# One latent weave re-filled, its layer norms cut into pieces, and the logits' wait on the copies narrowed, in a two-block transformer kernel on one core

## The reference

```python
def mixer_layer(x, cx, c, c_ctx, w_in, w_out, w_ada, b_ada, ln_g, ln_b, ...):
    shift, scale, gate = split(silu(c) @ w_ada + b_ada, 3)          # and the same for c_ctx
    h  = x * (1 + scale) + shift                                    # modulation, hc likewise
    (a_q, a_i, a_ff, a_fb, b_q, b_k, b_v, c_q, c_k, c_v, d_q, d_k, d_v, g_lat) = split(h @ w_in)
    y_a = hgrn2_mixer(...)       # gated linear recurrence, both directions
    y_b = global attention, normed and rotated q, k   (keys of latents and context)
    y_c = differential attention                       (the same)
    y_d = windowed attention with a sink               (the same)
    y = concat(y_a, y_b, y_c, y_d) * silu(g_lat)
    x_new = layer_norm(alpha * x + gate * (y @ w_out), ln_g, ln_b)
    # the context gets the same in the first layer only

def layer_norm(x, g, b):
    mu = mean(x); var = mean(square(x - mu))
    return (x - mu) * rsqrt(var + 1e-5) * g + b
```

## Time and profile before

| | |
|---|---|
| time, median of 3 runs | 1595.27 us (1594.75 to 1596.22) |
| the profiled execution | 1594.29 us, of which its span 1592.3 us |
| PE busy | 1465.8 us (92%), 8186 instructions |
| DVE busy | 544.5 us (34%) |
| ACT busy | 399.2 us (25%) |
| POOL busy | 145.9 us (9%) |
| mean granted TensorE clock | 0.958 of full speed |
| `two0`, first logits to last mix | 987.0 to 1231.0 us |
| end of `two0` to first projection of `two1` | 1231.0 to 1300.7 us |
| `two1` | 1300.7 us to the end of the span |

### The profile page before, as it was taken

How to read it: one execution, slowest core, us unless ns; L and a number is a source line. 1 busy time by engine, 2 the same in 40 slices (tenths; PEclk the granted TensorE clock), 3 DMA queues, 4 the chain that set the end, 5 groups by cost and what they waited for, 6 DMA issues and landing times. The chain is left out here.

```text
span 1592.3 us, 20238 instructions
## 1 busy us (share of the span) xinstructions
PE 1465.8 (92%) x8186; PEld 1186.5 (75%) x8186; DVE 544.5 (34%) x1273; ACT 399.2 (25%) x730; POOL 145.9 (9%) x191
## 2 busy tenths in 40 slices
PE   5999999999999999999999999998998969779875
PEld 2887887888878788888888887776776847556664
DVE  1352122102153233141454223355444121465331
ACT  2122122310212223333133222223333012232221
POOL 0111100000020210000110001213000001231000
PEclk9999999999999999999999999999997979889977
DMA  9544344454355444433332343542422314111100
GB/s 369 217 168 168 146 159 185 168 203 185 132 190 208 159 168 159 165 133 136 129 132 106 110 142 119 212 185 76 161 94 82 133 41 144 54 53 41 67 0 27
DMA packets 30764, 219.86 MB, mean 138 GB/s; under 512 B 3792, under 2 KB 3920, under 8 KB 4304
## 3 DMA queue, kind: packets, MB, share of 16 engines
q1 hardware_dynamic: 30672, 218.57, 37.1%
HBM read 217.51 MB, written 1.05 MB: 137 GB/s over the span
## 5 line engine op out<-in xcount | busy, mean ns | idle before, releaser
L812 PE MATMUL event<-u,ring 128*128 128x256 f32 x3200 | 722.0, 385 | 17.5 <-DVE u L1621 10.6
L812 PEld LDWEIGHTS event<-u,ring 128*128 128x128 f32 x3200 | 610.3, 193 | 121.1 <-issue 30.8
L805 PE MATMUL event<-ring,u 128*128 128x256 f32 (+1 forms) x704 | 150.6, 372 | 0.0
L805 PEld LDWEIGHTS event<-ring,u 128*128 128x128 f32 x704 | 128.6, 191 | 20.7 <-issue 4.6
L1159 ACT ACTIVATE region<-event 128x512 f32<-128x512 f32 x72 | 43.0, 597 | 317.9 <-PE event L812 317.7
L986 PE MATMUL event<-region,ring 128*128 128x256 f32 x544 | 119.1, 379 | 2.9 <-DVE region L1641 2.9
L986 PEld LDWEIGHTS event<-region,ring 128*128 128x128 f32 x544 | 102.8, 190 | 17.9 <-issue 4.2
L1195 ACT ACTIVATE S<-logits,stat 128x512 f32<-128x512 f32 (+2 forms) x160 | 83.8, 535 | 111.3 <-DVE stat L1520 92.0
L1827 POOL TENSOR_TENSOR raw<-raw,tables 128x512 f32<-128x512 f32 (+1 forms) x28 | 34.1, 1219 | 843.8 <-DVE turned L1485 530.7
L897 PE MATMUL logits<-region 64*128 64x256 f32 (+4 forms) x320 | 66.1, 515 | 36.5 <-ACT PT L1211 22.0
L961 PE MATMUL event<-region,ring 128*128 128x256 f32 x384 | 84.4, 380 | 0.0
(11 more groups left out here) (191 smaller groups left out, 1232.3 us busy)
## 6 DMA issues: line engine op xcount, KB each, us to landing
ring<-in_w SPq DMA_DIRECT2D x202, 1024.0 KB, 4.8
tables<-in_two SPq DMA_DIRECT2D x1, 1600.0 KB, 9.4
x<-in_x SPq DMA_DIRECT2D x1, 1024.0 KB, 17.6
x<-in_ctx SPq DMA_DIRECT2D x1, 1024.0 KB, 6.5
out<-x SPq DMA_DIRECT2D x1, 1024.0 KB, 3.9
tables<-in_one SPq DMA_DIRECT2D x1, 832.0 KB, 9.0
tables<-in_late SPq DMA_DIRECT2D x1, 512.0 KB, 5.7
consts<-in_common SPq DMA_DIRECT2D x1, 320.0 KB, 3.3
```

The source lines that it names most:

```text
L805: ins = mm(bank[:, t * 256:t * 256 + width], mem.u[:, q, k, t * P:(t + 1) * P], wt[:, k * 256:k * 256 + width], start=k == 0, stop=k == KB ...
L812: ins = mm(bank[:, j * 256:(j + 1) * 256], wt[:, k * 256 + j * P:k * 256 + j * P + P], mem.u[:, q, k, :], start=k == 0, stop=k == KB - 1)
```

## The change

Three parts.

**Scripts.** The fill of `two0` is laid out anew. `kk` and `vv` of the context leave the weave; `vv` now stands between `mean(0)` and `var(0)`, and `fv` and `kk` between `var(0)` and `feed(0)`, after the weave. The other projections are spread so that in the second half of the weave there is one after each logits or each turn up to logits(14). The context's layer norm and feed move from slots 7 to 11 to slots 11 to 14. The head norm of the context's keys (`sq`, `norm` of gk1) moves from slots 18 and 19 of `two0` into the start of `two1`, where the first logits now wait for it. The load of the `late` table follows `proj vv` of the context as before, and so moves with it.

**Layer norms in pieces.** The mean's matmuls wait for the four `out` drains one by one; centring and squares are four instructions of 128x512 instead of one of 128x2048, each signalled; the variance's matmuls take the squares pair by pair; the eight multiplications, the eight additions and the eight of `feed` each signal the next engine singly, and the first projection after a `feed` waits block by block. The final store is four DMAs of 256 KB, each after its two blocks.

**Logits.** `logits(n)` waits for `turns_copied` only where one of the jobs n-2 to n is of kind C (these exist in block one only).

```diff
     fill = [[] for _ in range(2 * len(jobs))]
-    for h, items in ((0, [proj("hq")]), (1, [proj("hi")]), (2, [proj("nq")]), (3, [("rot", "nq", 0)]), (4, [out(1)]), (5, [out(2)]),
-                     (6, [out(3)]), (7, [("mean", 1)]), (8, [proj("fk"), ("var", 1)]), (9, [proj("fq"), ("rot", "fk", 0)]),
-                     (10, [proj("fv"), ("rot", "fq", 0)]), (11, [("mod", "v1"), ("feed", 1, "v1")]),
-                     (12, [proj("g", 0, 0)]), (14, [proj("ff", 1)]), (15, [proj("fb", 1)]), (17, [proj("kk", 1)]),
-                     (18, [proj("hi", 1), ("sq", "gk1")]), (19, [("norm", "gk1")]), (20, [proj("g", 0, 1)]), (22, [proj("g", 0, 2)]), (24, [proj("g", 0, 3)]),
-                     (26, [proj("vv", 1)]), (28, [("silu", 0)]), (29, [("gate", 0, 0)])):
+    for h, items in ((0, [proj("hq")]), (2, [proj("nq")]), (3, [("rot", "nq", 0)]), (4, [out(1)]), (6, [proj("hi")]), (7, [out(2)]),
+                     (9, [proj("fk")]), (10, [out(3)]), (11, [("mean", 1), ("rot", "fk", 0)]), (12, [proj("fq"), ("var", 1)]),
+                     (13, [("rot", "fq", 0)]), (14, [proj("fv"), ("mod", "v1"), ("feed", 1, "v1")]), (15, [proj("ff", 1)]),
+                     (17, [proj("fb", 1)]), (19, [proj("g", 0, 0)]), (21, [proj("hi", 1)]), (23, [proj("g", 0, 1)]),
+                     (25, [proj("g", 0, 2)]), (27, [proj("g", 0, 3)]), (28, [("silu", 0)]), (29, [("gate", 0, 0)])):
         fill[h] += items
     for h, items in enumerate(latent_scan()):
         fill[3 + h] += items
-    for h, items in ((18, [("decay", 1)]), (19, [("prep", 1, "khat")]), (21, [("khatT", 1)]), (23, [("state", 1)])):
+    for h, items in ((20, [("decay", 1)]), (22, [("prep", 1, "khat")]), (24, [("khatT", 1)]), (26, [("state", 1)])):
         fill[h] += items
-    for g, h in enumerate((1, 3, 5, 7, 13, 16)):
+    for g, h in enumerate((1, 5, 8, 11, 16, 20)):
         fill[h] += group("v1", g)
         fill[h + 1].append(("ada", g, "v1"))
     s += weave(len(jobs), fill)
     s += [("sq", "f0"), proj("fk", 1), ("norm", "f0"), ("gate", 0, 1)] + [("out", i, (0,)) for i in range(4)]
-    return s + [proj("fv", 1), ("mean", 0), ("var", 0), ("feed", 0, "v1")]
+    return s + [("mean", 0), proj("vv", 1), ("var", 0), proj("fv", 1), proj("kk", 1), ("feed", 0, "v1")]
 
 
 def script_two1():
...
     s = [proj("kk"), proj("vv"), ("rot", "nk", 0), ("sq", "gk0"), proj("gq"), ("norm", "gk0"), ("sq", "gq0"), proj("ff"), proj("fb"),
-         ("rot", "gk", 0), ("norm", "gq0"), proj("hq"), ("rot", "gq", 0), ("decay", 0)]
+         ("rot", "gk", 0), ("norm", "gq0"), ("sq", "gk1"), proj("hq"), ("rot", "gq", 0), ("norm", "gk1"), ("decay", 0)]
...
 
-    eng.wait_ge(sems["x_normed"], w.at("x_normed", 0))
-    eng.dma_start(dram["out"], mem.x[:, 0, :, :]).then_inc(sems["stored"], 16)
-    eng.wait_ge(sems["stored"], 16)
+    for i in range(4):
+        eng.wait_ge(sems["x_normed"], w.at("x_normed", 2 * i + 2 - KB))
+        eng.dma_start(dram["out"][:, 2 * i:2 * i + 2, :], mem.x[:, 0, 2 * i:2 * i + 2, :]).then_inc(sems["stored"], 16)
+    eng.wait_ge(sems["stored"], 64)
...
                                 eng.wait_ge(sems["u_ready"], w.at("u_ready", k + 1))
+                            elif after is not None and j == 0:
+                                eng.wait_ge(sems["fed"], after + k + 1)
                             ins = mm(bank[:, j * 256:(j + 1) * 256], wt[:, k * 256 + j * P:k * 256 + j * P + P],
                                      mem.u[:, q, k, :], start=k == 0, stop=k == KB - 1)
...
-                fed[item[1]] = w.at("fed", sec.index(item) + 1)
+                fed[item[1]] = w.at("fed", KB * sec.index(item) + 1) - 1
...
-                eng.wait_ge(sems["turns_copied"], w.at("turns_copied", n - 1))
+                if "C" in [j.kind for j in sec.jobs[max(n - 2, 0):n + 1]]:
+                    eng.wait_ge(sems["turns_copied"], w.at("turns_copied", n - 1))
...
+                        if n == 0 and sec.name == "two1":
+                            eng.wait_ge(sems["normed"], w.at("normed", sec.index(("sq", "gk1")) + 1))
...
                 q = item[1]
-                if kind == "mean":
-                    ev = w.first[("out", 3, (q,))]
-                    eng.wait_ge(drained[ev % BANKS], w.fills(ev))
-                else:
-                    eng.wait_ge(sems["vsquares"], w.at("vsquares", sec.index(("mean", q)) + 1))
                 src = mem.x if kind == "mean" else mem.u
                 eng.wait_ge(drained[e % BANKS], w.fills(e - BANKS))
                 bank = mem.bank[e % BANKS]
                 for k in range(KB):
+                    if k % 2 == 0 and kind == "mean":
+
+                        ev = w.first[("out", k // 2, (q,))]
+                        eng.wait_ge(drained[ev % BANKS], w.fills(ev))
+                    elif k % 2 == 0:
+                        eng.wait_ge(sems["vsquares"], w.at("vsquares", 4 * sec.index(("mean", q)) + k // 2 + 1))
                     ins = mm(bank[:, 0:T], c["ones"], src[:, q, k, :], start=k == 0, stop=k == KB - 1)
                 ins.then_inc(full[e % BANKS], 1)
...
             elif kind == "mean":
-                n = sec.index(item) + 1
-                eng.wait_ge(sems["centred"], w.at("centred", n))
-                act(mem.u[:, item[1]], mem.x[:, item[1]], ACT.Square).then_inc(sems["vsquares"], 1)
+                q = item[1]
+                for i in range(4):
+                    n = 4 * sec.index(item) + i + 1
+                    two = slice(2 * i, 2 * i + 2)
+                    eng.wait_ge(sems["centred"], w.at("centred", n))
+                    act(mem.u[:, q, two, :], mem.x[:, q, two, :], ACT.Square).then_inc(sems["vsquares"], 1)
                 eng.wait_ge(sems["vsquares"], w.at("vsquares", n))
...
-                eng.wait_ge(sems["x_scaled"], w.at("x_scaled", n))
                 for k in range(KB):
                     beta = mem.par2[:, 0 if q else sec.layer, TWO_BETA + k:TWO_BETA + k + 1]
-                    ins = act(mem.x[:, q, k, :], mem.x[:, q, k, :], ACT.Identity, bias=beta)
-                ins.then_inc(sems["x_normed"], 1)
-                eng.wait_ge(sems["x_normed"], w.at("x_normed", n))
+                    eng.wait_ge(sems["x_scaled"], w.at("x_scaled", KB * (n - 1) + k + 1))
+                    act(mem.x[:, q, k, :], mem.x[:, q, k, :], ACT.Identity, bias=beta).then_inc(sems["x_normed"], 1)
+                eng.wait_ge(sems["x_normed"], w.at("x_normed", KB * n))
...
-                if tag == "v1":
-                    eng.wait_ge(sems["x_normed"], w.at("x_normed", sec.index(("var", q)) + 1))
+                n = KB * sec.index(item)
                 for k in range(KB):
-                    ins = ts(mem.u[:, q, k, :], mem.x[:, q, k, :], mod[:, KB + k, q:q + 1],
-                             mod[:, k, q:q + 1], ALU.mult, ALU.add)
-                ins.then_inc(sems["fed"], 1)
-                eng.wait_ge(sems["fed"], w.at("fed", sec.index(item) + 1))
+                    if tag == "v1":
+                        eng.wait_ge(sems["x_normed"], w.at("x_normed", KB * sec.index(("var", q)) + k + 1))
+                    ts(mem.u[:, q, k, :], mem.x[:, q, k, :], mod[:, KB + k, q:q + 1],
+                             mod[:, k, q:q + 1], ALU.mult, ALU.add).then_inc(sems["fed"], 1)
+                eng.wait_ge(sems["fed"], w.at("fed", n + KB))
...
                 eng.wait_ge(full[e % BANKS], w.fills(e))
                 ts(mem.mean[:, :], bank[:, 0:T], 1.0 / D, None, ALU.mult).then_inc(drained[e % BANKS], 1)
                 eng.wait_ge(drained[e % BANKS], w.fills(e))
-                tt(mem.x[:, q], mem.x[:, q], wide(mem.mean[:, :], KB), ALU.subtract).then_inc(sems["centred"], 1)
-                eng.wait_ge(sems["centred"], w.at("centred", n))
+                for i in range(4):
+                    two = mem.x[:, q, 2 * i:2 * i + 2, :]
+                    tt(two, two, wide(mem.mean[:, :], 2), ALU.subtract).then_inc(sems["centred"], 1)
+                eng.wait_ge(sems["centred"], w.at("centred", 4 * n))
             elif kind == "var":
                 q, n = item[1], sec.index(item) + 1
                 l = 0 if q else sec.layer
                 eng.wait_ge(sems["vrs_ready"], w.at("vrs_ready", n))
                 for k in range(KB):
-                    ins = stt(out=mem.x[:, q, k, :], in0=mem.x[:, q, k, :],
-                              scalar=mem.par2[:, l, TWO_G + k:TWO_G + k + 1], in1=mem.rs_x[:, :],
-                              op0=ALU.mult, op1=ALU.mult)
-                ins.then_inc(sems["x_scaled"], 1)
-                eng.wait_ge(sems["x_scaled"], w.at("x_scaled", n))
+                    stt(out=mem.x[:, q, k, :], in0=mem.x[:, q, k, :],
+                        scalar=mem.par2[:, l, TWO_G + k:TWO_G + k + 1], in1=mem.rs_x[:, :],
+                        op0=ALU.mult, op1=ALU.mult).then_inc(sems["x_scaled"], 1)
+                eng.wait_ge(sems["x_scaled"], w.at("x_scaled", KB * n))
 
     def pick_keys(w, qt):
 

```

10 lines of the change are left out of this document (5 added, 5 removed).

## The result

The changed kernel takes 1544.95 us (median of 4 runs, 1543.4 to 1546.11), the kernel before on the same chip 1595.01; the ratio is 0.9686, 95% interval 0.9669 to 0.9702. The profiled execution took 1544.14 us with a span of 1542.3. Of the 50.0 us that the span lost, 34.0 are idle time of PE (126.5 before, 1542.3 - 1449.8 = 92.5 now) and 16.0 are matmuls that run faster (1465.8 to 1449.8 us for the same 8186). Of the 34.0, 1.9 are scatter: PE's first matmul starts at 9.81 us before and at 7.94 now, and anywhere from 7.3 to 9.9 us in the fourteen traces.

What follows compares the result with a forecast made beforehand. TensorE, busy 92% of the span, was taken as the bound, with 126.5 us idle plus slow-clock matmuls to win. Terms 21.5 + 8 + 4 + 10.1 = 43.6 us less gave 1550.7 profiled, forecast 1551.5 us, range 1541 to 1565.

Steps and rivals of the forecast that it cites:

- A, the seam: Between `two0` and `two1`: projections placed around the layer norm's steps cover PE's stops, 21.5 us less, bounds 18.5 to 22.
- B, the weave of `two0`: New order of the fill removes stops at logits(11) and logits(15) and shortens middle ones: 8 us less, bounds -3 to 16.
- fits behind 6.9 us: In the weave of `two0`, a job's chain of maximum, exponentials and copy, about 5 us, is covered by one projection.
- The idle time that I named as a sign, near 12 us: PE's idle time expected in the weave of `two0`, with the longest stop ahead of mix(14), near 7 us.
- C, `two1`: Loosened copies' wait, less the loss from the head norm ahead of the decay: 4 us less, bounds 0 to 8.
- The loss at the start: Start of `two1`: head norm delays the decay 2.9 us, its scalings then run 1.7 us faster; net +1.2 on logits(1).
- The term that was mis-sized: In `two1`, the loosened wait gives back the copy's part of stops from logits(7) to logits(14): 4.3 us.
- D, the last layer norm: Kernel end: mean, centring, squares, additions and store in pieces overlap: 10.1 us less, bounds 7 to 12.
- the 5.7 that I took: Last layer norm, centring to variance: 5.7 of 10.7 us left, between 4.85 at 2.4 GHz and 7.75 at 1.2 GHz.
- rival 3: More clock comes back than counted, slow stretches in both weaves go too: another 5 to 8 us, 1545 us; 10%.
- Rival 2: The copies' wait only changes its name, mix or norm wait instead: 1558 us; 13%.
- Rivals 1, 4 and 5: Middle of `two0` collides, 1560 to 1566, 17%; recurrence loses step in `two0`, 1602, 1%; seam not covered, 1562, 3%.

Runs made afterwards that it cites:

- e3: The changed kernel with layer norms, feed and final store whole as before, keeping the new scripts and loosened wait: 1568.09 us.
- e1: The changed kernel with the old wait for the copies put back in front of every logits: 1563.1 us.
- e2: The kernel before with only the loosened wait of logits for the copies: 1585.29 us.
- e4: The kernel before with layer norms, feed and store in pieces, old scripts and old wait: 1573.91 us.
- e5: The changed kernel with the square and norm of gk1 right behind kk and vv in `two1`, ahead of the decay's wait: 1542.52 us.
- e8: The changed kernel with two items of slot 11 of `two0` swapped, the rotary of fk ahead of mean(1): 1546.29 us.

## Why the prediction was right, and where it was not

**A, the seam: right in size and mechanism** (21.4 for 21.5). No stop, clock 1.00, and e3 shows that the order does it without the pieces.

**B, the weave of `two0`: right sum, wrong account.** The stops in the middle came to 0.40, 2.10, 2.54, 1.47 and 0.55 us, 7.1 in all, where 7.3 were forecast, behind mean(1), variance(1) and the feed; the one at mix(14) is 6.69 where near 7 were. The step that failed is that the new order alone gives the 8, because a job's chain "fits behind 6.9 us". With the old wait, 3.7 of the 8.6 are gone (e1), with stops of 2.41 and twice 0.77 us for the copies in the new order. Without the pieces, to which the forecast gave no gain here, 5.4 are gone (e3), at the stops behind the context's layer norm. The order itself is worth 3.0 us beside the loosened wait (219.3 to 216.3, e2 to e3) and 6.4 beside the pieces (221.0 to 214.6, e4 to e1, all less vv and kk where they are in the stretch); it takes all three for the 8.6. That the sum came out is luck. The idle time that I named as a sign, near 12 us, was added up wrongly; my own 7.3 and near 7 make 14, and 14.6 were measured.

**C, `two1`: right sign, too small** (6.5 for 4). The loss at the start was +1.4 us up to logits(1) against +1.2, with the scalings at 1.76 us as assumed. The Trainium skill ("SBUF — State Buffer", section "SBUF: two separate sides") has GpSimd and certain operations of VectorE lock each other out at a shared port pair. The scalings agree, 1.76 us without POOL beside them and 3.47 in e5 with it, and so do the centrings of e8, 2.50 and 5.21. The term that was mis-sized is the wait: idle 5.6 to 7.5 us instead of 4.3, and 3.9 to 7.0 of slow matmuls that I kept in the bounds. Up to and with logits(7) the idle part is 1.7 us in the old order and 3.7 in the new one, where I had 1.05, since I let the level waits swallow the rest. In the net of the changed kernel the idle part alone shows, 26.0 to 19.8, as its busy time stayed at 131.0.

**D, the last layer norm: right** (11.2 for 10.1). Mean 1.1 for 1.0; centring to the end of the variance 10.7 to 5.25, so 5.5 for 5.0, as the matmuls ran at the full clock. They did so in ten of the eleven traces with the pieces; in e4 the same variance behind the same stop of 2.13 us took 5.38 us, so the 5.7 that I took, between the two levels, hedged against something that does occur. Additions 2.8 for 2.9; store 1.8 for 1.2. The fixed and variable cost of the Trainium skill ("DMA: Bandwidth & Descriptors", section "Anatomy of one DMA"), which the page gives for DMAs that GpSimd issues and not SyncE as here, had given an estimate of 1.8. The traces agree in the difference (3.9 less 2.1 us) and lie 0.5 us below it in both lengths. Its advice to batch DMAs to 1 MiB and more ("Bandwidth") would have cost that here: the transfer is the last thing in the kernel, and three quarters of it can go while the source is still being made.

**The rivals.** Split by kind, the forecast's 43.6 us are 33.4 of idle and 10.2 of slow matmuls (A 5.7, B 1.5 and 0.9, D 2.05 of the 2.9 between the two clock levels of its variance). Measured were 34.0 and 16.0, and from logits(1) of `two0` on 32.3 and 16.3. So the idle time was right in the sum, and nearly the whole miss of 6.4 us in the span is that more clock came back than I counted. That is the number of rival 3, which I gave 10%, but only half its mechanism: it has the slow stretches inside both weaves go. From logits(1) to logits(15) 2.2 us of them went in `two0`, about what I had booked for its weave, and 0.2 in `two1` (131.2 to 131.0 us). The rest came at the ends of the weaves and behind them, 2.3 and 2.5 us between logits(15) and the mean in the two sections (fk 8.90 to 8.03, the first `out` of `two1` 8.93 to 8.38 us) and 1 us at logits(0) of `two1`, and a few us of all this are scatter, since the granted clock of one and the same script differs between traces. Rival 2, that the copies' wait only changes its name, is false for the sum (e2: 9.8 us), true for the whole weave of `two0` in the old order (e2: 0.2 us), and true at single places of the changed kernel: at logits(10), (13) and (15) of `two1` 1.55 us are now waited for the exponentials. Rivals 1, 4 and 5 did not come. A slip of the last step: 1550.7 and the 0.98 us make 1551.7, not 1551.5.

**What stays open.** Why the busy time of one and the same script of `two1` is 126.3 us in one trace and 131.0 in another is not settled; nor why the norm ahead of the decay goes with 6 us of slow matmuls under the old wait, nor what the new order of `two0` is worth in its weave with neither the loosened wait nor the pieces.

## What to carry to other kernels

Cover first, then cut: where independent matmuls can be put between the halves of a layer norm they hide it whole or in pieces, and the pieces pay where there is nothing to put beside them, at the end of the kernel and inside a weave that is already full. A stop of TensorE is worth its length and what the clock adds behind it: the wait that stood with 22.0 us in twelve pieces gave back 6 us of idle and 4 of slow matmuls when it alone was loosened (e2), so the second part belongs in the sum and not only in the bounds, with bounds of its own: the same script's matmuls scatter by 4.7 us here. The same wait gave nothing in `two0`, where its stops only changed their names; so ask at each place what the engine would wait for next. Before a gain is booked on a new order, ask whether the order would give it with the old waits and without the other parts of the change too.

## What the runs showed of the hardware

Behind a stop of 2.92 us the next projection took 9.35 us, behind 2.16 us at the same place 7.17; yet the last layer norm's variance ran in 3.69 us behind a stop of 2.13 in the changed kernel's trace and in 5.38 behind the same stop in e4's. So the length of the last stop doesn't settle the clock alone. Four centrings of 128x512 on VectorE took 2.50 us, and 5.21 with a rotary and subtractions of GpSimd beside them (e8). The same program started its second block 3.0 us apart in two traces (986.5 and 989.5), and its executions spread over 1543.4 to 1549.0 us, so moves of 2 us are read here from stretches of the traces and not from the medians.
